# Last attention: the compressed steps share one PSUM bank, output rows stand under eighteen heads, weight pieces are rounded later, gelu works on turned units

## The reference, cut to what matters

```
kc = rmsnorm(compress(kv[:, :, 0], cmp_pos[0], cmp_w1[0], cmp_w2[0]), k_gain[0])   # 15 compressed keys a group
vc = compress(kv[:, :, 1], ...)            # compress: gelu(flat @ w1) @ w2, flat is 30 x 2048, w1 2048 x 256
p_c = masked_softmax(q . kc + bias_c)      # compressed branch: 256 x 15 logits a head
p_s, p_w                                   # selected and window branch: 256 x 256 logits a head each
o   = g0 * (p_c @ vc) + g1 * (p_s @ vs) + g2 * (p_w @ vw)
y_mem = softmax(q . mem_k) @ mem_v         # 4 heads
x   = x + concat([o, y_mem]) @ w_out       # the output rows, w_out 1024 x 1024
```

## Time and profile before

| | before |
|---|---|
| median of three runs | 1539.57 us (1536.43 to 1539.68) |
| profiled execution: time | 1537.14 us |
| profiled execution: span | 1535.4 us |
| TensorE busy | 1438.6 us (94%) |
| VectorE busy | 887.0 us (58%) |
| ScalarE busy | 684.2 us (45%) |
| mean granted TensorE clock | 0.953 |

### The profile page before, as it was taken

One profiled execution on the slowest core, in us unless ns is written; L12 is line 12 of the kernel. 1 busy time (PEld: TensorE's weight loads), 2 busy tenths in 40 slices (PEclk: granted clock), 3 DMA queues, 4 the chain that ended last, 5 costly groups with the idle time before them and its releaser, 6 DMA issues.

```text
span 1535.4 us, 24444 instructions
## 1 busy us (share of the span) xinstructions
PE 1438.6 (94%) x10298; PEld 1353.5 (88%) x10298; DVE 887.0 (58%) x1183; ACT 684.2 (45%) x985; POOL 182.1 (12%) x174
## 2 busy tenths in 40 slices
PE   7998999999799899999998959899999889899998
PEld 6997999999799799999986748899998778799997
DVE  6476655456546766555567563645547765474554
ACT  5544543435435345443456332444346543354442
POOL 2002210101200112100022100211112300010000
PEclk9999999999999999999999977899999977899999
DMA  8631365554463135765544431354554430245552
GB/s 228 188 110 55 111 194 191 192 167 149 123 180 110 56 110 190 236 199 179 192 125 150 164 110 49 111 198 165 185 200 137 139 117 1 71 137 188 182 191 83
DMA packets 159657, 225.10 MB, mean 147 GB/s; under 512 B 19081, under 2 KB 127625, under 8 KB 159548
## 3 DMA queue, kind: packets, MB, share of 16 engines
q1 hardware_dynamic: 159548, 223.55, 45.2%
HBM read 222.44 MB, written 1.09 MB: 146 GB/s over the span
## 4 chain that ended last, share of the span: by engine, by line
PE 83%; DVE 9%; issue 3%; ACT 3%; POOL 1%; DMA 0%; DVEq 0%; SPq 0%; ACTq 0%; POOLq 0%
PE ps L2338 17%; PE ps L2340 16%; PE ps L2339 16%; PE ps L2330 5%; PE ps L2331 4%; PE ps L2332 4%; PE ps L2617 2%; DVE xT L1425 2%; PE ps L2618 2%; PE ps L2619 2%; DVE w_lo L1401 2%; PE ps L2969 2%; ACT w_hi L797 2%; DVE h L1440 1%; PE ps L2851 1%
## 5 line engine op out<-in xcount | busy, mean ns | idle before, releaser
L1401 DVE TENSOR_TENSOR w_lo<-raw,w_hi 128x2048 fp32r<-128x2048 f32 (+4 forms) x209 | 478.5, 2294 | 286.5 <-ACT w_hi L797 284.0
L2338 PE MATMUL ps<-xT,w_hi 128*128 128x256 f32 x1600 | 462.6, 289 | 13.4 <-DVE w_lo L1401 6.9
L797 ACT ACTIVATE w_hi<-raw 128x2048 fp32r<-128x2048 f32 (+4 forms) x209 | 392.2, 1879 | 168.9 <-PE ps L2340 81.5
L2339 PE MATMUL ps<-xT,w_hi 128*128 128x256 f32 x1600 | 456.9, 286 | 0.0
L2340 PE MATMUL ps<-xT,w_lo 128*128 128x256 f32 x1600 | 456.8, 286 | 0.0
L2338 PEld LDWEIGHTS ps<-xT,w_hi 128*128 128x128 f32 x1600 | 311.4, 195 | 17.5 <-DVE w_lo L1401 13.5
L2339 PEld LDWEIGHTS ps<-xT,w_hi 128*128 128x128 f32 x1600 | 311.5, 195 | 0.5
L2340 PEld LDWEIGHTS ps<-xT,w_lo 128*128 128x128 f32 x1600 | 311.2, 194 | 0.0
L2338 PE MATMUL ps<-hT,w_hi 128*128 128x256 f32 x640 | 182.7, 286 | 5.4 <-DVE hT L1887 4.6
L2339 PE MATMUL ps<-hT,w_hi 128*128 128x256 f32 x640 | 182.1, 285 | 0.0
L2340 PE MATMUL ps<-hT,w_lo 128*128 128x256 f32 x640 | 182.0, 284 | 0.0
(11 more groups left out here) (330 smaller groups left out, 2072.5 us busy)
## 6 DMA issues: line engine op xcount, KB each, us to landing
raw<-in_w_up_dram SPq DMA_DIRECT2D x54, 1024.0 KB, 5.4
raw<-in_w_down_dram SPq DMA_DIRECT2D x54, 1024.0 KB, 5.0
raw<-in_w_gate_dram SPq DMA_DIRECT2D x22, 1024.0 KB, 5.4
raw<-in_w_in_dram SPq DMA_DIRECT2D x14, 1024.0 KB, 5.5
raw<-in_a_w_in_dram SPq DMA_DIRECT2D x10, 1024.0 KB, 5.6
raw<-in_w_o_dram SPq DMA_DIRECT2D x8, 1024.0 KB, 5.0
raw<-in_w_ple_gate_dram SPq DMA_DIRECT2D x8, 1024.0 KB, 5.0
raw<-in_w_out_dram SPq DMA_DIRECT2D x8, 1024.0 KB, 4.9
```

The lines of the kernel that those rows point to most:

```text
L797: nc.scalar.activation(w_hi[:, p % RH, 0:piece_width(p)], raw[:, p % RR, 0:piece_width(p)], ACT.Copy).then_inc(E["hi_ready"], 1)
L1401: nc.vector.tensor_tensor(w_lo[:, p % RH, 0:w], raw[:, p % RR, 0:w], w_hi[:, p % RH, 0:w].bitcast(F32), ALU.subtract).then_inc(E["lo_ready ...
L2338: nc.tensor.matmul(out_, w[0][:, kk, c], x(0, k), start=start and j == 0, stop=False, skip_group_check=True)
L2339: nc.tensor.matmul(out_, w[0][:, kk, c], x(1, k), start=False, stop=False, skip_group_check=True)
```

## The change

1. **Banks.** All compressed steps use bank 1 in turn (before: 1, 6, 7, 4, 5); the hidden units of key and value lie in banks 4 and 6. The weights of the two token blocks are turned in steps 16 and 17 instead of both in 16, and the three compressed outputs are in steps 18, 20, 21 instead of 17, 18, 19.
2. **Output rows.** Banks 4 to 7 are then free from step 8 on. The output rows begin in step 10 instead of 20 and are one to four units a head; eight of the 48 units stand behind the last head, around `turned_pair(4)`.
3. **Pieces.** The piece behind q chunk 0 is rounded in step 1 instead of ahead of step 0, the next in step 2 instead of 1, those of `cmp` 1 in steps 12 and 18 instead of 6 and 7, that of `w_out` 0 in step 20 instead of 22. The pair of memory heads is turned in step 6 instead of 12.
4. **Gelu.** The raw units are copied out and turned first (step 8, four transposes into bank 1), and square, polynomial, Exp and reciprocal work on 128x120 instead of 30x512.

```diff
-        ROWS_2 = 20
-        BESIDE_2 = ((0, 0, 6), (0, 6, 11), (0, 11, 16), (1, 0, 6), (1, 6, 11), (1, 11, 16), (2, 0, 8), (2, 8, 16))
+        ROWS_2 = 10
+        BESIDE_2 = ((0, 0, 2), (0, 2, 4), (0, 4, 6), (0, 6, 8), (0, 8, 10), (0, 10, 11), (0, 11, 12), (0, 12, 13), (0, 13, 14),
+                    (0, 14, 16), (1, 0, 4), (1, 4, 7), (1, 7, 10), (1, 10, 13), (1, 13, 16), (2, 0, 3), (2, 3, 6), (2, 6, 8))
-        GROUP_OUT = (1, 2, 3, 4, 8, 9, 10)
-        COMP_OUT = (5, 6, 7)
+        GROUP_OUT = (1, 2, 3, 4, 6, 9, 10)
+        COMP_OUT = (5, 7, 8)
...
-                wide_evac(("q", 0), 512, z1[:, :, 0:512], ("mix", 1))
+                wide_evac(("q", 0), 512, z1[:, :, 0:512], ("mix", 1), ahead_=False)
...
                     if i == 1:
-                        used(("q", 1), 0)
+                        used(("q", 0), 1)
                     if i == 2:
                         evac_units(query_units(0))
+                        used(("q", 1), 0)
...
                     if i == 6:
                         evac_units(query_units(1))
-                        used(("cmp", 1), 0)
+                        rounded_pair(6)
                     if i == 7:
                         hidden_units(1)
-                        used(("cmp", 1), 1)
                     if i == 8:
+                        act.wait_ge(E["zeroed"], 1)
+                        act.wait_ge(E["gel_t"], 1)
+                        nc.scalar.activation(hfun, PS[1][:, 0:120], ACT.Square).then_inc(E["gel_sq"], 1)
+                    if i == 9:
                         act.wait_ge(E["gel_u"], 1)
...
                     if i == 12:
-                        rounded_pair(6)
+                        used(("cmp", 1), 0)
...
+                    if i == 18:
+                        used(("cmp", 1), 1)
                     if i == 19:
                         rounded_pair(0)
+                    if i == 20:
+                        used(("w_out", 1), 0)
                     if i == 22:
                         rounded_pair(2)
-                        used(("w_out", 1), 0)
...
-                    if i in (17, 18, 19):
-                        compressed_out(4 * (i - 17))
+                    if i in (18, 20, 21):
+                        compressed_out({18: 0, 20: 4, 21: 8}[i])
...
-                    if i in (12, 19, 22):
-                        pe.wait_ge(E["o_evac"], G0 + {12: 1, 19: COMP_OUT[0], 22: GROUP_OUT[4]}[i])
-                        if i == 12:
-                            pe.wait_ge(E["rep_done"], 1)
-                        turned_pair({12: 6, 19: 0, 22: 2}[i])
+                    if i in (6, 19, 22):
+                        pe.wait_ge(E["o_evac"], G0 + {6: GROUP_OUT[0], 19: COMP_OUT[0], 22: COMP_OUT[2]}[i])
+                        turned_pair({6: 6, 19: 0, 22: 2}[i])
...
                 values(NL - 1)
+                out_rows(2, 8, 12)
                 pe.wait_ge(E["o_evac"], G0 + 10)
                 turned_pair(4)
+                out_rows(2, 12, 2 * KD)
```

More of the change, by code:

```diff
@@ L1052, in wide_evac @@
                         after_()
-                    split_upto(last + RH)
+                    if ahead_:
+                        split_upto(last + RH)
                     p = last
```

121 lines of the change are left out of this document (61 added, 60 removed).

## The result

The changed kernel took 1527.78 us (median of 4 runs, 1526.5 to 1528.11), the kernel before 1538.78: ratio 0.9929, 95% interval 0.9912 to 0.9946, so 11.0 us gained. The forecast was 1516 us. It was worked out from the profiled 1537.14 us as 24.7 us saved less 4 for the clock, 20.7 us gained, so about half of the gain came. The time lies at the upper edge of the range, in the rival "clock stays low for long".

A forecast was written before the change was run, and what follows sets the result against it. TensorE, busy 94%, bounds the kernel; only its waits and half clock can give time. Savings of 4.8 + 20.3 - 0.35 = 24.7 us from 1537.14 give 1512.4, plus 4 for clock falls: 1516 us, range 1507 to 1528.

The forecast's parts named there:

- clock stays low for long: Rival, chance 0.19: light heads keep TensorE at half clock, 10 to 20 us over 1512, so 1522 to 1532.
- the price of the clock: Two falls of about 4 us at half clock behind the new waits, 2 us each: 4 us lost.
- part b: Heads 8 to 27: gaps and half clock removed, units moved, less 8.65 us of new waits; 20.3 us saved.
- the slower rival: Rival, chance 0.04: clock falls in head 13 and nothing lifts it before the tail; +43 us, 1555.
- 376 to 386: Earlier trace window with 2.55 us idle, mean clock 0.83, 3.4 us at half; taken as a model for clock recovery.
- The large waits: New TensorE waits from VectorE's order: 2.25 us in head 13, 1.55 in head 19, 2.6 around heads 20 and 21.
- The small ones: Small new waits at heads 9, 10, 16, 20 and 22, 2.25 us together.
- Part a: Start of the last attention: rounding moved into head 1, less wait and half clock before first transposes; 4.8 us saved.
- The second remainder in heads 1 to 3: Extra VectorE remainder of 2.29 us, mostly covered; 0.75 us of new wait at head 4.
- The gelu: Heads 8 to 11: reciprocal falls from 3.34 to 0.90 us, chain hidden, so gaps and 20.0 us of half-clock loss go.
- Part c: Tail, last values to last blocks: eight units fill the gap, about 9 us in all; 0.35 us lost.
- The shared bank: Rival, chance 0.02: about twelve hand-overs in bank 1 at 2.75 us each eat the gain; time the same.

The follow-up runs named there:

- f1_behind: Changed kernel, wait in head 13 kept, with four output-row units each in heads 14 and 15 and none in heads 16 to 19; 1526.27 us.
- e5_best: Changed kernel with VectorE remainders moved to heads 13 and 21, ScalarE rounding to head 24, compressed outputs ahead of moves, last pair's rests ahead of the remainder; 1502.19 us.
- b2_start: Kernel before with only the start changed: rounding behind the first q chunk moved into head 1, the next into head 2; 1535.93 us.
- e6_rowslate: Changed kernel with all output rows back under heads 20 to 27, so heads 8 to 19 are bare and none stand behind the last; 1535.09 us.
- g4_late_nogap: g3_rows_nogap with all output rows under heads 20 to 27, none behind the last head, w_out roundings kept in heads 22 and 25; 1523.31 us.
- g3_rows_nogap: e5_best with the rounding in head 12 moved to head 13 on ScalarE, and the remainder to head 14 on VectorE; 1501.15 us.
- h1_bare14: g3_rows_nogap with heads 14 to 17 bare, their five units moved into heads 18 and 19; 1508.12 us.
- f4_gap15: e5_best with the second piece's remainder in head 13 ahead of the scaling of the turned keys, not behind it; 1510.68 us.
- f3_clean12: e5_best with the second piece's remainder back in head 12, ahead of the closing of group 2; 1513.08 us.
- h2_bare12: g3_rows_nogap with heads 12 and 13 bare, their four units moved into heads 14 to 16; 1505.80 us.
- g1_bare_nogap: g3_rows_nogap with heads 12 to 17 bare, their units moved into heads 18 and 19 (six each); 1512.70 us.
- g2_bare_gap: e5_best with heads 12 to 17 bare, units moved into heads 18 and 19, ScalarE's rounding left in head 12; 1515.32 us.
- e4_bare: Changed kernel with the second piece's remainder in head 13 and no units in heads 12 to 17, their eight moved to heads 18 and 19; 1528.63 us.

## Why the prediction was wrong

**The step that failed** is the price of the clock: "I take two falls of about 4 us at half, 2 us each: 4." There were two falls in part b, but the first was 20.4 us at half, 10.2 us of time, and the second 3.4 us, 1.7: 11.9 in place of 4, which is 7.9 of the 8.6 us that part b fell short. The reason given there, "both stretches had wide products behind the gap, as the heads from 10 on have", was the mistake. Heads 14 to 18 hold one or two units each; f1_behind, with four in heads 14 and 15, still took over 13 us. The sentence under the slower rival, that heads with three or more units ran at 1.00, read more out of the earlier trace rows than is there: the heads of that window hold five to eight units. The nearest rows were not 376 to 386, but the 38.4 us at 0.50, the same heads' work on the same engine. The rival built on them (0.19; 10 to 20 us over 1512) had the price right.

**The large waits were sized right, their sum by luck.** Head 13: 2.14 (2.25 forecast); head 19: 1.56 (1.55); head 21: 2.83 (2.6). The small ones came to 0.65 in heads 9 and 20, not 2.25, and 1.41 stands in heads 26 and 27, which I had not seen: ScalarE's rounding of head 25 ahead of exponentials (with it in head 24, e5_best has neither gap). The sum, 8.6 for 8.65, is so near only because this made up for the small ones.

**Part a** was right in the changed kernel: first transposes 3.66 us behind the first scores (6.70 before), clock 1.00 behind them, 4.5 saved where I had 4.8. The second remainder in heads 1 to 3 cost gaps of 0.27 and 0.47. b2_start, without the pair, saved 5.0 us in the same part, and the program gained 2.5.

**The gelu** was right in size (0.90 us) and hidden, with no gap over 0.2 us in heads 7 to 11, and the bare heads 8 and 9 ran at 1.00. Its value was not: I had booked 20 us of half clock (40 us long) as gone with the gap. In e6_rowslate, rows late and the new gap in head 13 kept, the clock was still at half for 41 us. In g4_late_nogap, rows late and no gap over 0.7 us ahead of the last pair, it was for 27, and the gain was 14.4 us; with the rows spread as well (g3_rows_nogap) it was 36.5. Terms that are each priced alone and added up were the wrong form: what closing a gap gives back depends on the load around it.

**Part c** was right: 9.17 us, about 9 forecast. That much of it is an order that can be turned round, I read past: in e5_best it is 4.2 us from the last values to the last blocks (1302.07 to 1306.31).

**The shared bank.** The Trainium skill (Perfetto Trace Analysis, "Optimizing Tensor Performance") advises independent matmul groups to rotate through the banks, and the prediction priced that rule as a rival. The trace bears it out at one of some twelve hand-overs, 2.83 us in head 21, where the compressed product waits for its bank alone. The pair in head 19 (1.56 us) is turned into bank 1 too, but it also needs the compressed output itself in `xs`, so another bank would not have spared that wait. The others cost 0.65 us in all, where 2.25 were charged. No run gives the steps banks of their own again.

**The cause now**: in these runs the clock falls where TensorE is given little to do for a while, and both gaps and light heads bring it down. Bare heads alone lower it (h1_bare14 against g3_rows_nogap, one edit apart). Among heads of one or two units a gap of 1.5 or 2.2 us lowers it (f4_gap15, f3_clean12), and gaps of 0.4 to 0.5 us in heads 19 and 20 don't (e5_best). In the changed kernel a gap of 1.56 us in head 19, with two units beside it and four in the next head, did not lower it; one of 2.83 in head 21 did. How long it stays varies with what follows: with one or two units a head 14 and 20 us (f4_gap15, f3_clean12), with four 14 (f1_behind), and 7 where the gap was 0.69 (h2_bare12). With none it came back in five kernels only behind the first unit, 1.4 to 3.7 us behind it, after 17 to 41 us (h1_bare14, g1_bare_nogap, g2_bare_gap, e4_bare, e6_rowslate), and in g4_late_nogap in head 19, before any unit, after 27. These are single executions; how far the stay varies between executions of one kernel no trace shows. Open is why bare heads 8 to 12 hold (g4_late_nogap, e6_rowslate) and 13 or 14 don't. The narrow compressed products of heads 11 and 14 may be part of it; no kernel here varies them.

## What to carry to other kernels

Where TensorE's work is light, price a new gap not by its length but by the half clock behind it: here 1.5 to 2.2 us of waiting cost 8.5 to 11. Read the length of the stay from a stretch with the same kind of work, not from another gap of the same size, and take it as a range (14 to 20 us here). Before adding up what an earlier start or a removed gap gives, look whether the stretch behind would keep the clock: here an earlier start was worth 2.5 us, the start with the gelu and the bank 3.3, two waits taken out of the changed kernel 0, and one remainder in another place 9.8. The whole with every gap closed gained 36 us, and the nearest kernel without the spread rows 14: spreading independent products under the light steps is what makes much of the rest count.
